# High and low part of the activations side by side: two of three weight passes as one 512-column matmul

## What is computed

```
for layer in range(2):
    h = h + 0.5 * swiglu(rms_norm(h), w_gate, w_up, w_down)    # width 2816
    u = rms_norm(h) @ w_in          # layer 0: gated conv of 31 taps; layer 1: causal attention
    h = h + concat([primary, memory_attention(q_mem, mem)]) @ w_o
    h = h + 0.5 * swiglu(rms_norm(h), ...)
swiglu(x) = (silu(x @ w_gate) * (x @ w_up)) @ w_down
# third block: one input projection, differential attention (4 heads) and an mLSTM
# (4 heads), two gates, projections w_a and w_b, out = rms_norm(merged @ w_out) + h
```

## Time and profile before

| | us |
|---|---|
| median of 3 runs (lowest, highest) | 1316.06 (1311.69, 1316.13) |
| the profiled execution | 1311.87 |
| its span, first to last instruction | 1310.6 |
| TensorE matmul busy | 1263.4 |
| DVE busy | 859.8 |
| ACT busy | 636.7 |
| mean granted TensorE clock | 0.986 |

### The profile page before, as it was taken

One profiled execution on the slowest core, in us unless ns is written; L12 is line 12 of the kernel. 1 busy time (PEld: TensorE's weight loads), 2 busy tenths in 40 slices (PEclk: granted clock), 3 DMA queues, 4 the chain that ended last, 5 costly groups with the idle time before them and its releaser, 6 DMA issues.

```text
span 1310.6 us, 22985 instructions
## 1 busy us (share of the span) xinstructions
PE 1263.4 (96%) x9684; PEld 1218.7 (93%) x9684; DVE 859.8 (66%) x1287; ACT 636.7 (49%) x945; POOL 60.0 (5%) x84
## 2 busy tenths in 40 slices
PE   7999999986999999999999998899999999999998
PEld 6999999975999999999999987799999999878997
DVE  6575566888666555666555667565565668666986
ACT  5444445562654444454444446554444443556363
POOL 3000000010000000000000123000000000000000
PEclk9999999988999999999999999999999998999999
DMA  8665555510456555665555555045665564645440
GB/s 272 224 195 179 181 180 180 174 52 1 138 184 186 181 173 178 196 181 181 178 181 178 166 176 164 1 129 178 182 183 170 177 188 153 190 128 159 151 159 35
DMA packets 193188, 211.72 MB, mean 162 GB/s; under 512 B 8976, under 2 KB 180112, under 8 KB 193086
## 3 DMA queue, kind: packets, MB, share of 16 engines
q1 hardware_dynamic: 190480, 206.66, 50.5%
q10 hardware_dynamic: 2606, 3.60, 0.8%
HBM read 209.19 MB, written 1.05 MB: 160 GB/s over the span
## 4 chain that ended last, share of the span: by engine, by line
PE 87%; DVE 9%; ACT 2%; POOL 1%; issue 1%; DMA 0%; SPq 0%; ACTq 0%; DVEq 0%; POOLq 0%
PE psum L439 85%; DVE wlo L1612 2%; DVE cv L1785 2%; POOL small L2351 1%; PE psum L780 1%; PE psum L569 1%; ACT pb L1513 0%; DVE small L1894 0%; DMA xn<-in_x 0%; DVE small L2069 0%; ACT pb L1359 0%; DVE pb L2079 0%; POOL small L2350 0%; PE psum L597 0%; DVE xl L1679 0%
## 5 line engine op out<-in xcount | busy, mean ns | idle before, releaser
L1612 DVE TENSOR_TENSOR wlo<-raw,whi 128x1024 fp32r<-128x1024 f32 (+2 forms) x403 | 471.0, 1189 | 269.4 <-ACT whi L1107 269.1
L439 PE MATMUL psum<-xh,whi 128*128 128x256 f32 x1952 | 556.8, 285 | 3.8 <-ACT whi L1107 2.4
L439 PE MATMUL psum<-xl,whi 128*128 128x256 f32 x1952 | 554.0, 284 | 0.7 <-DVE xl L1690 0.7
L439 PE MATMUL psum<-xh,wlo 128*128 128x256 f32 x1952 | 553.8, 284 | 0.8 <-DVE wlo L1612 0.8
L1107 ACT CAST whi<-raw 128x1024 fp32r<-128x1024 f32 (+2 forms) x403 | 401.9, 1020 | 304.7 <-PE psum L439 300.6
L439 PEld LDWEIGHTS psum<-xh,whi 128*128 128x128 f32 x1952 | 375.9, 193 | 5.0 <-ACT whi L1107 2.8
L439 PEld LDWEIGHTS psum<-xl,whi 128*128 128x128 f32 x1952 | 376.0, 193 | 1.1 <-DVE xl L1690 1.1
L439 PEld LDWEIGHTS psum<-xh,wlo 128*128 128x128 f32 x1952 | 375.8, 193 | 1.1 <-DVE wlo L1612 1.1
L439 PE MATMUL psum<-gh,whi 128*128 128x256 f32 x704 | 197.1, 280 | 0.0
L439 PE MATMUL psum<-gh,wlo 128*128 128x256 f32 x704 | 196.8, 280 | 0.0
L439 PE MATMUL psum<-gl,whi 128*128 128x256 f32 x704 | 196.2, 279 | 0.0
(11 more groups left out here) (297 smaller groups left out, 980.5 us busy)
## 6 DMA issues: line engine op xcount, KB each, us to landing
raw<-in_ffn_w_gate SPq DMA_DIRECT2D x88, 512.0 KB, 4.7
raw<-in_ffn_w_up SPq DMA_DIRECT2D x88, 512.0 KB, 4.5
raw<-in_ffn_w_down SPq DMA_DIRECT2D x80, 512.0 KB, 4.4
raw<-in_w_in SPq DMA_DIRECT2D x52, 512.0 KB, 3.5
raw<-in_w_o SPq DMA_DIRECT2D x16, 512.0 KB, 3.4
raw<-in_a_w_in SPq DMA_DIRECT2D x14, 512.0 KB, 4.6
raw<-in_w_kv SPq DMA_DIRECT2D x16, 384.0 KB, 3.2
raw<-in_ffn_w_down SPq DMA_DIRECT2D x16, 256.0 KB, 2.7
```

The costliest lines, as they stand in the source:

```text
L439: return pe.matmul(o, l, r, start=start, stop=stop, skip_group_check=True)
L1612: dve.tensor_tensor(B.wlo[:, i % SPLIT, 0:n], B.raw[:, i % RAW, 0:n], B.whi[:, i % SPLIT, 0:n].bitcast(F32), ALU.subtract).then_inc(*s.lo. ...
```

## The change

Activations. `xh`/`xl` and the FFN's `gh`/`gl` become two halves of one buffer, the high part's 256 columns followed by the low part's. A block becomes two matmuls: the high weight tile with all 512 columns, which fills a whole bank, and the low weight tile with the first 256 columns, which adds to the left half. The result is the sum of a bank's two halves. Each output half j now has a bank of its own, so a pair of them takes two banks where it took one, and the FFN uses banks 0 and 1 for every gate and 2 and 3 for every up. An engine reads at most one operand of that kind from PSUM here: ACT copies the right halves to SBUF (`half`), then DVE adds the left halves to them (`halves`), and only then comes the scaling that used to read PSUM directly. The residual adds (`add_h`) are two DVE adds in a row. The GAB slots are cut the other way: 128 output columns and all eight k, one bank each. The WA sums move up to directly behind each WA slot, ahead of the transposes of the mLSTM output.

```diff
+    B.x = [sb(f"x{i}", [128, 8, 2, S], F32R) for i in range(2)]      # xh = x[:, :, 0], xl = x[:, :, 1]
+        F.g = sb(f"g{f}", [128, 22, 2, S], F32R, c)                  # gh, gl likewise
-    for c in range(8):
-        narrow(win, 8, 4616 + c * 256)
+    for c in range(16):
+        plan.append((win, 0, 8, 4616 + c * 128, 128))
# TensorE
+    def block(b, h, l, x, start, stop, ready=None):
+        mm(bank[b], h, x.rearrange("p a b -> p (a b)"), start, False)
+        if ready is not None:
+            pe.wait_ge(*s.lo.at(ready))
+        return mm(bank[b][:, 0:S], l, x[:, 0, :], False, stop)
@@ cols (down alike)
+                if first:
+                    first_use(s.x_hi, gen, kc)
+                    first_use(s.x_lo, gen, kc)
-                    mm(o, h[:, k, q], x[0][:, kc, :], kc == 0 and j == 0, False)
-                    mm(o, h[:, k, q], x[1][:, kc, :], False, False)
-                    t = mm(o, l[:, k, q], x[0][:, kc, :], False, last)
+                    t = block(b + j, h[:, k, q], l[:, k, q], x[:, kc], kc == 0, kc == K - 1, ...)
@@ ffn
-            if p >= 2:
-                pe.wait_ge(*s.gate.at((f, p - 2)))
+            if p:
+                pe.wait_ge(*s.sum.at(("gate", f, p - 1)))
-            if p >= 2:
-                pe.wait_ge(*s.mul.at((f, p - 2)))
+            if p:
+                pe.wait_ge(*s.sum.at(("up", f, p - 1)))
@@ second
+            if c >= 2:
+                pe.wait_ge(*s.sum.at(("qk", c - 2)))
...
+                pe.wait_ge(*s.sum.at(("gab", c - 2)))
...
+            if c >= 2:
+                pe.wait_ge(*s.sum.at(("wa", c - 2)))
...
+            if c >= 2:
+                pe.wait_ge(*s.sum.at(("wb", c - 2)))
# ScalarE
+    def half(key, slot, out, b):
+        act.wait_ge(*s.used.at(slot))
+        act.copy(out, psum[:, b:b + 2, S:2 * S]).then_inc(*s.half.now(key))
# VectorE
+    def halves(key, out, b):
+        dve.wait_ge(*s.half.at(key))
+        dve.tensor_tensor(out, psum[:, b:b + 2, 0:S], out, ALU.add).then_inc(*s.sum.now(key))
+        dve.wait_ge(*s.sum.at(key))
@@ ffn: per pair p
+                if i == 0 and p:
+                    up_out(p - 1)          # halves(up), wait silu, multiply
+                if i == 1 and p:
+                    up_rest(p - 1)         # low part
+                if i == 2:
+                    gate_sum(p)            # halves(gate)
+                    if p:
+                        gate_scale(p)
                 use(base + 4 * p + i)
@@ ffn: after each group of down
+            halves(("down", f, p), tmp, (4, 6, 0, 2)[p])
+            dve.scalar_tensor_tensor(out=tmp, in0=tmp, scalar=0.5, in1=row, ...)
@@ add_h
+        for half in range(2):
+            t = dve.tensor_tensor(pair, psum[:, b:b + 2, half * S:(half + 1) * S], pair, ALU.add)
@@ rest, 16 GAB slots
+            dve.wait_ge(*s.half.at(("gab", c)))
+            dve.tensor_tensor(g, b[:, 0:S], g, ALU.add).then_inc(*s.sum.now(("gab", c)))
+            dve.wait_ge(*s.sum.at(("gab", c)))
+            dve.tensor_tensor(g, g, row_of(6), ALU.mult).then_inc(*s.gab.now(c))
@@ second, WA
         for c in range(4):
             use(WA2 + c)
+            g = flat(MC.ga[:, 2 * c:2 * c + 2, :])
+            tmp = B.htmp[:, c % 2, :]
+            halves(("wa", c), in_pairs(tmp), 2 * (c % 2))
+            dve.wait_ge(*s.gab_act.at(c // 2))
+            dve.tensor_tensor(g, g, tmp, ALU.mult).then_inc(*s.u.now(("a", c)))
         for tt in range(2):
             turned("yb", tt, 4, 1, 4, [4 + tt])
```

More of the change, by code:

```diff
@@ L298, in signals @@
     jobs2 = [("d", i) for i in range(8)] + [("m", i) for i in range(8)]
+    sums = []
+    for f in range(4):
+        for p in range(PAIRS):
+            sums += [("gate", f, p), ("up", f, p)]
+        sums += [("down", f, p) for p in P4]
+        if f == 0:
+            sums += [(k, p) for p in range(3) for k in ("a", "g")]
+    for k, n in (("qk", 4), ("aqk", 4), ("gab", 16), ("wa", 4), ("wb", 4)):
+        sums += [(k, c) for c in range(n)]
     s.w = [sig(f"w_in{i}", range(i, SLOTS, RAW), 16) for i in range(RAW)]
@@ L384, in signals @@
     s.act_step = steps("act_step")
+    s.half = sig("right_half", sums)
+    s.sum = sig("halves_sum", sums)
     s.lo = sig("w_lo", range(SLOTS))
@@ L465, in side, with cols @@
             short_taps()
-    def cols(x, first, K, slot, b, gen=None, g0=0):
+    def block(b, h, l, x, start, stop, ready=None):
[3 more added lines that the diff above has]
+        return mm(bank[b][:, 0:S], l, x[:, 0, :], False, stop)
+    def cols(x, first, K, slot, b, gen=None):
         i = slot
@@ L615, in ffn @@
                 pe.wait_ge(*s.x_lo.at(("mem0", 1, 1)))
-            if f == 1 and p == 2:
+            if f == 1 and p == 1:
                 pe.wait_ge(*s.kT0.at((1, 1)))
-            down(f, F, base + 44 + 6 * p, 4 + p, p == 0)
+            if p == 2:
+                pe.wait_ge(*s.sum.at(("gate", f, PAIRS - 1)))
+            if p == 3:
+                pe.wait_ge(*s.sum.at(("up", f, PAIRS - 1)))
+            down(f, F, base + 44 + 6 * p, (4, 6, 0, 2)[p], p == 0)
     def down(f, F, slot, b, first):
@@ L667, in mix_a @@
         X0, X1 = (xh[0], xl[0]), (xh[1], xl[1])
+        pe.wait_ge(*s.h.at((1, 2)))
         for p in range(3):
[L669 to L673, removed]
+            if p:
+                pe.wait_ge(*s.sum.at(("a", p - 1)))
+            cols(B.x[0], p == 0, 8, AIN + 4 * p, 0, "m0")
+            if p:
+                pe.wait_ge(*s.sum.at(("g", p - 1)))
+            else:
+                pe.wait_ge(*s.h.at((1, 3)))
+            cols(B.x[0], False, 8, AIN + 4 * p + 2, 2)
         cp = conv_steps()
@@ L907, in rest @@
             else:
[L908 to L923, removed]
-                t.then_inc(*s.used.now(i))
-                yield
+                pe.wait_ge(*s.sum.at(("gab", c - 2)))
+            i = GAB2 + c
+            h, l = weights(i, 8, 128)
+            pe.wait_ge(*s.hi.at(i))
+            for k in range(8):
+                t = block(6 + c % 2, h[:, k, :], l[:, k, :], x[:, k], k == 0, k == 7, i if k == 0 else None)
+            t.then_inc(*s.used.now(i))
+            yield
     def weights_turn2(st, i):
@@ L1455, in rest @@
                 yield
-        for c in range(8):
-            for k in range(2):
-                use(GAB2 + 2 * c + k)
-                yield
+        for c in range(16):
+            use(GAB2 + c)
+            act.wait_ge(*s.used.at(GAB2 + c))
+            act.copy((MC.ga if c < 8 else MC.gb)[:, c % 8, :], bank[6 + c % 2][:, S:2 * S]).then_inc(*s.half.now(("gab", c)))
+            yield
     def z_rows(i):
@@ L1488, in second @@
         use(GATE2)
-        for i in range(8):
-            use(AQK2 + i)
+        for c in range(4):
+            for i in range(2):
+                use(AQK2 + 2 * c + i)
+            if c >= 2:
+                act.wait_ge(*s.c_dve.at(f"aqk{c - 2}"))
+            half(("aqk", c), AQK2 + 2 * c + 1, in_pairs(B.htmp[:, c % 2, :]), 2 * (c % 2))
         for h in range(2):
@@ L1736, in ffn, with gate_sum, gate_scale, up_out @@
         v = (1, 3, 4, 6)[f]
+        row = wide(row_of(n), 1, 2)
+        def gate_sum(p):
+            halves(("gate", f, p), in_pairs(F.gr[:, p % 2, :]), 0)
+        def gate_scale(p):
+            r = in_pairs(F.gr[:, p % 2, :])
+            if p == 0:
+                dve.wait_ge(*s.row.at(n))
+            dve.tensor_tensor(r, r, row, ALU.mult).then_inc(*s.gate.now((f, p)))
+        def up_out(p):
+            r, q = F.gr[:, p % 2, :], F.pr[:, p % 2, :]
+            halves(("up", f, p), in_pairs(q), 2)
+            dve.wait_ge(*s.silu.at((f, p)))
+            dve.tensor_tensor(q, r, q, ALU.mult).then_inc(*s.mul.now((f, p)))
@@ L1765, in ffn @@
             prep(v, p, targets)
     def add_h(v, p, slot, b, targets):
-        pair = flat(hT[:, 2 * p:2 * p + 2, :])
+        pair = hT[:, 2 * p:2 * p + 2, :]
         dve.wait_ge(*s.used.at(slot))
-        dve.tensor_tensor(pair, bank[b], pair, ALU.add).then_inc(*s.h.now((v, p)))
+        for half in range(2):
+            t = dve.tensor_tensor(pair, psum[:, b:b + 2, half * S:(half + 1) * S], pair, ALU.add)
+            if half == 0:
+                t.then_inc(*s.dve_step.tick())
+                dve.wait_ge(*s.dve_step.last())
@@ L1771, in add_h @@
+        t.then_inc(*s.h.now((v, p)))
         prep(v, p, targets)
```

259 lines of the change are left out of this document (147 added, 112 removed).

## The result

The changed kernel takes 1318.72 us in the median of ten runs (1312.65 to 1323.80), the kernel before 1312.12; the ratio is 1.0042, 95% interval 1.0022 to 1.0063. So it is about half a percent slower. Its profiled execution is one of its quickest: span 1313.2 us, 2.6 more than before.

The account below looks back on a forecast made before the run. TensorE bounds the kernel (87% of the chain of waits, DVE 9%). Terms -11.1 + 5.4 + 5.5 + 5.4 + 2.0 = +7.2 us give execution 1319.1, raised toward the runs' median to 1321 us; range 1302 to 1337.

Parts of the forecast that it names:

- The block, 353 ns: TensorE's block of 512 plus 256 columns takes 353 ns, not 360 in `cols`; gain 11.1 us over 1664 blocks.
- Rival A: Everywhere on the path a block takes 347 ns or less; kernel faster, 1305 us; chance 0.30.
- `down`, gain nothing: Down projections: a block took 353.4 ns before and would take 353, so no gain.
- The middle of an FFN at nothing: Inside FFNs the added copies and sums cost nothing, covered by two slots (5.7 us) before banks are reused.
- Rival D: In FFN pairs DVE and ACT make TensorE wait, 0.5 us in each of 44 pairs; 1343 us; chance 0.06.
- Stage starts, 5.4 us: Starts of FFNs and AIN, plus convolution and QK: added sums delay TensorE, 5.4 us lost, bounds 2 and 9.
- mLSTM, 5.5 us, bounds 4 and 9: mLSTM loop: DVE is full, and each GAB slot's add and scaling make it 5.5 us longer.
- WA, 5.4 us: WA: only two slots fit the banks, so later ones wait for DVE's sums; 5.4 us more, bounds 3 and 8.
- rival E: Longer gap before WA's third and WB's first slot drops the clock, some 3 us at half pace; 1324 us; chance 0.07.
- WB and OUT, 2.0 us: WB and OUT: DVE's longer turn per group and late last splits cost 2.0 us, bounds 0 and 4.
- B: The forecast itself: blocks take 353 ns, 1321 us, own range 1314 to 1328; chance 0.45.
- The second test: Forecast is wrong if the stretch from the mLSTM loop's start to the end is less than 8 us longer.

Follow-up runs that it names:

- dn: Changed kernel with the down projections alone in their old form (three passes, one bank, no copy or sum); 1318.88 us, ratio to before 1.0050.
- fill: Changed kernel with 28 unread filler matmuls ahead of WA's third slot and 16 ahead of WB's first; 1318.08 us, ratio to before 1.0038.
- gab: Changed kernel with the eight GAB products alone in their old form; 1315.72 us, ratio to before 1.0021.
- best1: Changed kernel with WO of both layers, GAB, WA and WB in the old form; 1306.42 us, ratio to before 0.9954.
- split: Changed kernel with the 512-column matmul again two of 256, layout, copies and sums kept; 1339.91 us, ratio to before 1.0204.
- best3: `best2` with the mixer's first product in old form and the norm's variance ahead of the first sum at the FFNs; 1297.59 us, ratio to before 0.9886.
- best2: `best1` with the down projections in their old form too; 1301.94 us, ratio to before 0.9918.

## Why the prediction came out as it did

The time and the sign were right, 1321 us and slightly slower, for a sum whose two sides were both too small and offset each other: the blocks gave 20 to 21 us where the forecast had 11.1, and the rest cost 27 where it had 18.3. That the two misses cancel was luck, and so was the last step. The forecast's profiled execution was to take 1319.1 us and took 1314.4 and 1311.8, a change of 2.6 and -0.1 us where the sum had 7.2. It added 2.1 us to get to the median, from three runs of the kernel before; ten runs of that kernel have their median only 0.3 us over the profiled execution, while the changed kernel's lies 4 to 8 us over its own.

- **The block, 353 ns, "I take 353".** Wrong as a single value. Both readings were right: the alternating stream ran at 353, the arithmetic of the earlier trace rows gives 346 to 347, and the kernel does either, by stretches. The gain was 20 to 21 us, not 11.1. By my own test (wrong under 349 ns) the step failed for two thirds of the `cols` blocks in the profile. (The 349 ns at which gain and losses were to cancel counts `cols` alone; with the 704 blocks of `down` it is 350.3.) Rival A had the price right for those; it did not win, because the losses were larger too.
- **`down`, gain nothing.** 2.7 us at TensorE in the profile, and nothing in all (`dn`), for its sums cost as much.
- **The middle of an FFN at nothing.** Right: its matmuls have no idle time before them but at the starts, and the FFNs gained about what the block predicts. Rival D is out.
- **Stage starts, 5.4 us.** The right mechanism: by TensorE's rows 0.8 + 0.8 + 1.0 + 0.1 us at the first norm and behind three FFNs (by the table's marks 0.8 + 1.5 + 1.0 + 0.8), and putting the norm first took 2.4 us of waits away. Missed was WO of layer 0: I had its blocks only among those that gain, while DVE's turn of 6.12 us is longer than TensorE's 5.65 and makes the next start late. The mixer with WO lost 1.5 us (by the marks 2.1), of which 0.8 came back with WO in its old form.
- **mLSTM, 5.5 us, bounds 4 and 9.** 3.0 to 4.4 us; DVE's step 8.03 where I had about 8.1. The mechanism was right and the term too high, at or under its lower bound.
- **WA, 5.4 us.** The step as worked out was exact: 11.4 us from the normalisation to WB, 11.3 where the clock stays up (`fill`). What failed is that it stood without rival E, to which I gave 0.07: behind the longer wait the clock drops, the blocks take 640 ns, and the third and fourth sums wait for them. That is 2.7 us before WB and 3.0 to 4.4 in the tail, where E had some 3.
- **WB and OUT, 2.0 us.** 2.3.
- **Chances.** B and A were not rivals but two levels of one stream; a mixture of both with E is what ran. The second test, 8 us more from the mLSTM loop to the end, held: the tail alone is 11.8 us longer.

By the formula of the Trainium skill ("TensorE: Matmul & The Clock Gate", section Back-to-back issue gap) the pair would, as an estimate, be at 325 ns and the gain at 2.5 ns a block. The trace disagrees on both: 346.7 or 353.3, and 6.7 or 13.3 ns. The prediction also left out that the section gives this formula for an isolated matmul and has a figure of its own for a stream of weight loads and matmuls, about 131 ns for 512 columns; the stream of the earlier trace rows, at 226 ns, does not show that either.

## What to carry to other kernels

A matmul over both halves of the operand pays where TensorE sets the pace and another engine has time to read and add two halves. Choose it stage by stage: here FFN gate and up gained, QK and AQK gained about 1 us (`gab`), and the same form cost time in WA and GAB and, as far as `best1` tells, in WB and WO. Where a change doubles the banks that a product holds, count how many products fit before the first reader comes, as that wait cost twice here: the wait, and the clock behind it. And put what a whole stage waits for ahead of the new reading in the reader's list.

## What the runs showed of the hardware

- A steady stream of weight load and matmul repeated at one of a few distances, 346.7, 348.9 or 353.3 ns for 512 + 256 columns, held it over up to hundreds of blocks and changed, where it did, when other matmuls came between or a down projection began. The same program showed 353.4 and 346.7 ns at the same place in two executions. What selects the level stays open.
- Three matmuls of 256 columns took 360.0 ns in `cols`, both in the kernel before, with the two parts in separate tiles, and in `split`, with them side by side; so the layout is not the reason. In `down` they took 353.3 ns in these two and in `dn`, but 350.0 in the third down projection of `best3` and 340.0 in the fourth of `best2` and `best3`. So three passes have several levels too, and what selects them stays open.
- In the tail a wait of TensorE of 4.2 to 4.3 us was followed by a granted clock of 0.50, the 1.2 GHz level, in both profiles of the changed kernel. With 28 idle-filling matmuls in its place, a wait of 0.6 us was left and the clock stayed at 1.00.
- In layer 1's attention the same instructions ran at 1.00 in some executions and for some 10 us at 0.50 in others, with 3 to 4 us more time. What decides it stays open.
- The longer runs of the changed kernel are those with the lower mean clock, about 12 us for 0.01 over its twenty runs. Whether the clock is the cause or a companion, no run here settles.
